# A hybrid decoder step on one core: modulation rows one unit sooner, last gate unit chunk by chunk, weight places in another order

## The reference

```
mod = silu(c) @ w_ada + b_ada                  # six pieces: shift, scale, gate, twice
h = rmsnorm(x) * (1 + sc1) + sh1
u, q, k, v, ga, gb = split(h @ w_in)
A = pool_mix(u) ; B = window_attention(q, k, v)
x = x + gt1 * ((sigmoid(ga) * (A @ w_a) + sigmoid(gb) * (B @ w_b)) @ w_out)
h2 = rmsnorm(x) * (1 + sc2) + sh2
x = x + gt2 * (relu(h2 @ w_up)**2 @ w_down)
y = rmsnorm(x)
```

## Time and profile before

| | |
|---|---|
| median of three runs | 1319.77 us |
| the profiled execution's own time | 1318.88 us |
| its span, first to last instruction | 1317.1 us |
| PE busy | 1278.0 us, 97% |
| DVE, ACT, POOL busy | 62%, 43%, 14% |
| mean granted PE clock | 0.993 of full speed |

### The profile page before, as it was taken

One profiled execution on the slowest core, in us unless ns is written; L12 is line 12 of the kernel. 1 busy time (PEld: TensorE's weight loads), 2 busy tenths in 40 slices (PEclk: granted clock), 3 DMA queues, 4 the chain that ended last, 5 costly groups with the idle time before them and its releaser, 6 DMA issues. The chain is left out here.

```text
span 1317.1 us, 24641 instructions
## 1 busy us (share of the span) xinstructions
PE 1278.0 (97%) x10185; PEld 1248.4 (95%) x10185; DVE 819.6 (62%) x1222; ACT 571.4 (43%) x984; POOL 189.1 (14%) x186
## 2 busy tenths in 40 slices
PE   6999999999999999998999999999999999999996
PEld 5899999999989999998889999999999999999996
DVE  7611446654333655347798877676768885688864
ACT  5322323454443633326666655555553434334332
POOL 1000100000000122222423332322320000000001
PEclk9999999999999999999999999999999999999999
DMA  9988422222222543543335554535398756676533
GB/s 308 317 275 277 152 65 66 72 86 71 66 66 74 175 132 102 153 141 111 94 121 156 163 161 154 164 123 158 122 335 250 250 179 234 213 222 207 181 129 100
DMA packets 238556, 211.59 MB, mean 161 GB/s; under 512 B 16145, under 2 KB 219797, under 8 KB 233565
## 3 DMA queue, kind: packets, MB, share of 16 engines
q1 hardware_dynamic: 237580, 209.66, 50.3%
q10 hardware_dynamic: 865, 0.36, 0.1%
HBM read 161.97 MB, written 49.04 MB: 160 GB/s over the span
## 5 line engine op out<-in xcount | busy, mean ns | idle before, releaser
L542 PE MATMUL psum<-xh,b_hi 128*128 128x264 f32 x908 | 257.9, 284 | 5.9 <-DVE b_lo L1658 3.6
L544 PE MATMUL psum<-xh,b_lo 128*128 128x264 f32 x908 | 257.9, 284 | 0.0
L543 PE MATMUL psum<-xl,b_hi 128*128 128x264 f32 x908 | 256.5, 282 | 0.0
L542 PE MATMUL psum<-dh,e_hi 128*128 128x264 f32 x896 | 255.3, 285 | 1.1 <-DVE e_lo L1658 1.0
L543 PE MATMUL psum<-dl,e_hi 128*128 128x264 f32 x896 | 254.0, 283 | 0.0
L544 PE MATMUL psum<-dh,e_lo 128*128 128x264 f32 x896 | 253.9, 283 | 0.0
L542 PE MATMUL psum<-h_hi,w_hi 128*128 128x384 f32 (+1 forms) x624 | 208.7, 334 | 5.2 <-DVE h_lo L1387 2.4
L543 PE MATMUL psum<-h_lo,w_hi 128*128 128x384 f32 (+1 forms) x624 | 202.1, 324 | 0.0
L544 PE MATMUL psum<-h_hi,w_lo 128*128 128x384 f32 (+1 forms) x624 | 201.9, 324 | 0.0
L542 PEld LDWEIGHTS psum<-xh,b_hi 128*128 128x128 f32 x908 | 170.5, 188 | 7.7 <-DVE b_lo L1658 4.9
L543 PEld LDWEIGHTS psum<-xl,b_hi 128*128 128x128 f32 x908 | 170.6, 188 | 0.0
(11 more groups left out here) (295 smaller groups left out, 2384.2 us busy)
## 6 DMA issues: line engine op xcount, KB each, us to landing
down_raw<-in_w_down_dram SPq DMA_DIRECT2D x72, 512.0 KB, 5.6
dr<-ff_scratch SPq DMA_DIRECT2D x28, 1056.0 KB, 8.3
up_raw<-in_w_up_dram SPq DMA_DIRECT2D x76, 256.0 KB, 3.8
ff_scratch<-st SPq DMA_DIRECT2D x64, 264.0 KB, 3.4
ada_p<-in_w_ada_dram SPq DMA_DIRECT2D x8, 2048.0 KB, 9.7
ff_scratch<-st SPq DMA_DIRECT2D x32, 396.0 KB, 3.5
w_raw<-in_w_in_dram SPq DMA_DIRECT2D x22, 512.0 KB, 5.2
gates_scratch<-g_out SPq DMA_DIRECT2D x16, 528.0 KB, 3.2
```

The lines of the kernel that those rows point to most:

```text
L542: mm(out, whi, rhi, start=first, stop=False)
L543: mm(out, whi, rlo, start=False, stop=False)
L544: return mm(out, wlo, rhi, start=False, stop=last)
```

## The change

**Start.** Pair 1's rows move from ahead of chunk 1 to between the two units of chunk 0, and their transpose moves to behind the first tile of the second unit. DVE's `by_token` steps are spread: two instead of three at first, then two, then one behind each lo. Of chunks 3 and 5 the normed value `nrm` is made by ACT (a new activation with the new semaphore `n_whole`) instead of DVE. ACT's row copies of pairs 1 to 3 stand ahead of chunks 2, 4 and 6 instead of 2, 3 and 5. The state row's transfer shares the semaphore of the vectors.

**Last gate unit.** `last_gate` goes chunk by chunk in the order 0, 4, 1, 5, 2, 6, 3, 7: six chunks through all three tiles, each with a signal `gate_left`, then the last two per tile. `turn_probs` stands behind the second chunk, `weigh` behind the fourth. ACT and DVE make the branch halves as the chunks of `h` become free, and ACT's three gate copies stand behind six of the eight hi copies.

**Weight places.** `down_place` exchanges the places 1 and 2 of the down weights.

```diff
+def down_place(k):
+    return (0, 2, 1, 3, 4)[k % 5]
+LAST_GATE = (0, 4, 1, 5, 2, 6, 3, 7)
+S_ORDER = (0, 1, 2, 4, 5, 6, 3, 7)
...
@@ PE, start @@
-                if k in (1, 2, 4):
+                if k in (2, 4):
                     pair_rows(k // 2 + 1)
                 for s in range(2):
+                    if (k, s) == (0, 1):
+                        pair_rows(1)
...
-                        if (s, t) == (0, 0) and k in (1, 2, 4):
+                        if (k, s, t) == (0, 1, 0):
+                            pair_turn(1)
+                        if (s, t) == (0, 0) and k in (2, 4):
                             pair_turn(k // 2 + 1)
@@ PE, last gate unit @@
+            def last_gate(i, u):
+                whi, wlo = weights(u)
+                for t in range(3):
+                    wait(pe, free[t], take(t, ("g", u, t)))
+                for n, k in enumerate(LAST_GATE[:6]):
+                    for t in range(3):
+                        last = mm3(psum[:, t, 0:TW[t]], ..., n == 0, False)
+                    last.then_inc(gate_left, 1)
+                    if n == 1:
+                        turn_probs(i, 1)
+                    if n == 3:
+                        weigh(i)
+                for t in range(3):
+                    for k in LAST_GATE[6:]:
+                        last = mm3(psum[:, t, 0:TW[t]], ..., False, k == LAST_GATE[7])
+                    last.then_inc(ready[t], 1)
...
@@ ACT, start @@
+                if k in (3, 5):
+                    act.wait_ge(h_done, k - 1)
+                    fn(nrm[:, k % 2, :], xn[:, k, 0:TP], ACT.Identity, scale=..., bias=...).then_inc(n_whole, 1)
@@ ACT, last gate unit @@
+            def branch_hi(k):
+                if k % 4 == 3:
+                    there(last_of[W_AB - 1])
+                else:
+                    act.wait_ge(gate_left, LAST_GATE.index(k % 4) + 1)
+                fn(hi, src, ACT.Copy).then_inc(s_hi_done, 1)
...
@@ DVE, start @@
-            for j in range(3):
+            for j in range(2):
                 by_token(j)
...
                 pair_add(p)
                 norm(2 * p)
-                norm(2 * p + 1)
+                if p == 3:
+                    norm(7)
                 norm_lo(2 * p)
                 norm_samples(p)
+                if p < 3:
+                    by_token(2 * p + 2)
                 norm_lo(2 * p + 1)
+                if p < 3:
+                    by_token(2 * p + 3)
@@ SP, down weights @@
-                        if up_place(m) // 2 == k:
+                        if up_place(m) // 2 == down_place(k):
                             when_released(*released(UP_RAW[m], False)[0:2])
```

More of the change, by code:

```diff
@@ L771, in pool_map @@
                     mm3(psum[:, t, 0:TW[t]], wp_hi[:, g, :], wp_lo[:, g, :], d_hi[:, cols(t)], d_lo[:, cols(t)], True, True).then_inc(ready[t], 1)
+            def last_gate(i, u):
[4 more added lines that the diff above has]
+                    for t in range(3):
+                        last = mm3(psum[:, t, 0:TW[t]], whi[:, k, :], wlo[:, k, :], h_hi[:, k, cols(t)], h_lo[:, k, cols(t)], n == 0, False)
+                    last.then_inc(gate_left, 1)
[5 more added lines that the diff above has]
+                    for k in LAST_GATE[6:]:
+                        last = mm3(psum[:, t, 0:TW[t]], whi[:, k, :], wlo[:, k, :], h_hi[:, k, cols(t)], h_lo[:, k, cols(t)], False, k == LAST_GATE[7])
+                    last.then_inc(ready[t], 1)
+                last_of[u] = ("g", u, 2)
             for i in range(BLK):
@@ L1011, in _ @@
                     split_hi(1)
+                if k in (3, 5):
+                    act.wait_ge(h_done, k - 1)
+                    fn(nrm[:, k % 2, :], xn[:, k, 0:TP], ACT.Identity, scale=gain1[:, k, 0:1], bias=mod[:, k, 0:1]).then_inc(n_whole, 1)
             split_hi(2)
@@ L1122, in gate_sig @@
                 fn(g_in[:, j % 2, :, :], g_in[:, j % 2, :, :], ACT.Sigmoid).then_inc(sig_done, 1)
-            there(last_of[W_AB - 1])
+            def branch_hi(k):
[3 more added lines that the diff above has]
+                    act.wait_ge(gate_left, LAST_GATE.index(k % 4) + 1)
+                hi, src = (a_hi[:, k, :], z[:, U0 + k, :]) if k < 4 else (o_hi[:, k - 4, :], z[:, Q0 + k - 4, :])
+                fn(hi, src, ACT.Copy).then_inc(s_hi_done, 1)
             for t in range(3):
                 freed(("pool", NG - 1, t))
-            for k in range(4):
-                fn(a_hi[:, k, :], z[:, U0 + k, :], ACT.Copy).then_inc(s_hi_done, 1)
-            freed(("o", BLK - 1))
-            for k in range(4):
-                fn(o_hi[:, k, :], z[:, Q0 + k, :], ACT.Copy).then_inc(s_hi_done, 1)
+            branch_hi(0)
+            pt_copy(BLK - 1, 1)
+            branch_hi(1)
+            done = there(("o", BLK - 1))
+            fn(z[:, Q0:Q0 + G, (BLK - 1) * P:TP], psum[:, 7, :].rearrange("p (c t) -> p c t", c=G), ACT.Copy).then_inc(done, 1)
+            branch_hi(2)
+            freed(("o", BLK - 1))
+            for k in (4, 5, 6):
+                branch_hi(k)
+            for t in range(3):
+                gate_copy(BLK - 1, 1, t)
+            for k in (3, 7):
+                branch_hi(k)
             split_hi(W_AB + 1)
@@ L1413, in _ @@
             norm_lo(1)
[L1414 removed]
+            for j in (2, 3):
                 by_token(j)
             for p in range(1, DK // 2):
[L1417 to L1419 removed]
                 pair_add(p)
                 norm(2 * p)
[L1422 removed]
+                if p == 3:
+                    norm(7)
                 norm_lo(2 * p)
                 norm_samples(p)
+                if p < 3:
+                    by_token(2 * p + 2)
                 norm_lo(2 * p + 1)
+                if p < 3:
+                    by_token(2 * p + 3)
             split_lo(2)
@@ L1553, in _ @@
                     nc.vector.tensor_copy(pool_tail[:, :, :].rearrange("p g (b r) -> p g b r", b=NB), pool_s[:, :, :, NT:PAD + NT]).then_inc(tail_done, 1)
-            for k in range(8):
-                dve.wait_ge(s_hi_done, k + 1)
+            for n, k in enumerate(S_ORDER):
+                dve.wait_ge(s_hi_done, n + 1)
+                if k % 4 == 3:
+                    there(last_of[W_AB - 1])
+                else:
+                    dve.wait_ge(gate_left, LAST_GATE.index(4 + k % 4) + 1)
                 src, hi, lo = (z[:, U0 + k, :], a_hi[:, k, :], a_lo[:, k, :]) if k < 4 else (z[:, Q0 + k - 4, :], o_hi[:, k - 4, :], o_lo[:, k - 4, :])
@@ L2194, in _ @@
                     if k < 3:
-                        at_step = max(released(UP_RAW[m], False)[2] for m in range(len(UP_RAW) - 6, len(UP_RAW)) if up_place(m) // 2 == k)
+                        at_step = max(released(UP_RAW[m], False)[2] for m in range(len(UP_RAW) - 6, len(UP_RAW)) if up_place(m) // 2 == down_place(k))
                     else:
```

31 lines of the change are left out of this document (19 added, 12 removed).

## The result

The changed kernel took **1309.91 us** (median of 4 runs, 1309.47 to 1311.97), the kernel before 1319.73 (4 runs, 1319.3 to 1321.25): ratio 0.9927, 95% interval 0.9909 to 0.9944. That is 9.8 us less; 7.2 were forecast. Run once more on another occasion the changed kernel took 1309.23 (five runs, 1309.03 to 1312.88). The profiled execution took 1309.54 us, its span 1307.7.

The account below looks back on a forecast made before the run. PE, busy 97% of the span, was taken as the bound, gaining only at waits and slow clock. Start 2.0 + last gate unit 4.2 + weight places 1.0 = 7.2 us: 1311.7 profiled, forecast median 1312.5, range 1310.5 to 1315.

Parts of the forecast that it names:

- range of 8 in 10: Whole kernel: the wider forecast range for the time, from 1309.9 to 1317.0 us.
- signs that would have shown it wrong: Pair 1 wait over 4 us, 1.2 GHz beyond 41.4, over 1 us wait at last gate unit or first product, feed-forward wait growing.
- The start: First units: 2.38 us wait at chunk 6 goes, 0.4 lost at pair 1's rows; 2.0 us gained, range 0.5 to 2.4.
- the other term: Start, pair 1's rows: PE waits 2.4 us instead of 0.94, chunk 1 starts late; 0.4 us lost.
- The case of a full clock: Start: if the clock were still full when pair 1's rows start, chunk 1 would start at 38.7.
- rival A: Start gives nothing: pair 1 lands late or its wait keeps the clock down; 1314.3 us, chance 0.16.
- D: Start: clock stays at 1.2 GHz through the chunks to 57.8, up to 19.8 us more; 1332 us, chance 0.05.
- The last gate unit: Behind the last gate unit: 2.81 us wait and slow clock go, 0.2 taken off; 4.2 us gained, range 1.5 to 4.5.
- Its two terms: Last gate unit: 2.81 us wait goes, and 3.2 us at 1.2 GHz did work of 1.6; together 4.4 us.
- Rival B: Behind last gate unit: gates return too late, PE waits 1.7 us for bank 3; 1314.0 us, chance 0.09.
- Rival C: Last gate unit: waits of 2 to 3 us return, clock falls again; gain 3.0 in all, 1316.8 us, chance 0.10.
- Weight places: Down product, second step: load issued earlier, PE's 1.02 us wait goes; 1.0 us gained, range 0 to 1.1.

Follow-up runs that it names:

- start_only: Kernel before with only the start's changes (pair 1's rows, by_token, nrm, row copies, joined semaphore): 1315.56 us, ratio 0.9970.
- halves_late: Changed kernel, ACT making all eight hi halves only after the last gate unit and gate copies, order 0, 1, 2, 4, 5, 6, 3, 7: 1316.04 us.
- busy_out: Changed kernel plus 28 identity transposes meant for the output product's wait, but placed where PE doesn't wait (524.34): 1314.06 us, ratio 0.9962.
- halves_plain: Changed kernel, all eight hi halves only after the last gate unit and gate copies, in order 0 to 7: 1313.53 us, ratio 0.9959.
- gate_only: Kernel before with only the last gate unit chunk by chunk and the branch halves in the places it leaves: 1314.05 us, ratio 0.9958.
- down_only: Kernel before with only places 1 and 2 of the down weights exchanged: 1318.16 us, ratio 0.9993.
- busy_out_2: Changed kernel plus 34 identity transposes inside PE's 3.97 us wait for wo_lo in the output product: 1311.93 us, ratio 0.9949.

## Why the prediction was right

The direction, the places and the mechanisms were right. The size was short by 2.6 us of 9.8 in the medians, and that the time still fell in the range of 8 in 10, by a hundredth of a us, is luck. None of the signs that would have shown it wrong came.

**The start: right in kind, too small (2.0 against 3.6).** The 2.38 us wait at chunk 6 went, by the chain the prediction named: the copy behind chunk 5's hi. With the copies put back it returns, as three smaller waits. The prediction put the lo's end at 56.5 and PE's need at 58.2; they were 54.85 and 56.66, the spare 1.8 as forecast. The failed size is the other term, 0.4 us lost at pair 1's rows: it was 0.75 gained at chunk 1, and 0.2 more with pair 1's turn, which is through by then. The wait ahead of them was 3.14 us, not 2.4, with the transfer landed at 34.2 instead of 33.8; but they ran in 1.95 us, not 3.24, because the clock was at 2.4 GHz where the prediction, from the earlier trace rows, had it at 1.2 until 38. The case of a full clock was also summed wrong, at 38.7 for chunk 1: half of the 3.24 and half of the 2.9 behind 33.8 give 36.9.

That the slow stretch would stay in its place rested on one execution. Of the seven profiled executions with the whole new start, five show no fall there, two a fall of 3.4 us right behind the wait for pair 1; of the three with the old start one shows 6.8 us and two 3.4. The traces tell how much of the 1.6 us not forecast is a matter of execution. The third unit begins at 62.0 to 63.8 in the seven, 62.8 in the mean, and at 64.8 to 66.0 in the three, 65.6 in the mean. So the start is worth about 2.8 us, half way between the forecast 2.0 and the 3.6 of the first pair of traces; the slow clock in that one execution of the kernel before makes up part of the rest. The median of start_only gives 3.8, its trace 2.6.

**Rivals A and D** speak of the clock at the start. A (no gain there, 1314.3) and D (slow clock through the chunks, 1332) did not come in the result, though the wait that was to cause them did, longer than forecast. The 3.4 us of slow clock of rival A did come in halves_late and busy_out; in halves_late it cost 1.3 us at the third unit (63.76 against 62.45).

**The last gate unit: right, 4.05 against 4.2.** The idle of 2.81 became 0.22, where the prediction had none, and the clock behind it is at 2.4 GHz. The 0.2 that it took off was for PE's wait for the bank of the first gate product; PE doesn't wait there. halves_plain gives 4.1 for the halves alone, the same number from the other side. Its two terms stand too: halves_late shows a wait of the same 2.81 without the fall, halves_plain with it. The first sigmoid came at 432.80. Before it was at 438.41; the shift of PE is 7.63, so against PE the gates are 2.0 us later. The prediction said 434.4, which with the start's further 1.6 is 432.8. Rival B needed PE to be ready for DVE before the gates are; the sigmoid ended at 434.77 and DVE took PE's bank at 435.59, so the bank was the later of the two by 0.8 us. Rival C needed holes of 2 to 3 us inside the unit; there are none.

**Weight places: right, 1.0 against 1.3.** The e_lo wait went, and 1.28 us with it: the wait of 1.02 and what PE takes to be back at its pace behind it. The load that was issued at 961.14 and took 12.3 us is now issued at 948.44, 12.7 us sooner, or 5 against PE's shift of 7.7. By issues (name, engine, KB, us to landing) it takes:

```profile
down_raw<-in_w_down_dram SPq DMA_DIRECT2D x1, 512.0 KB, 10.9
```

It lands at about 959.4, and its hi is made at 961.04. The 0.34 us at the first matmul of the down product are not part of it, as start_only and gate_only show. The Trainium skill, "DMA: Bandwidth & Descriptors", Queues, rings and completion order, has each engine take its descriptors in ring order, and the prediction read from it that what is passed gets later, without loss. The rows agree. The two transfers of 1056 KB that it passes are issued at 952.32 and 954.86 and take 10.4 and 10.5 us, to 962.7 and 965.4; before they were issued at 960.03 and 960.40 and landed at 969.5 and 972.1, which is 0.9 to 1.0 sooner once PE's shift of 7.7 is taken off. ACT first takes them up at 971.14, with no wait for them:

```profile
970.17 1.06 ACT L1244 ACTIVATE e_hi<-down_raw 128x1024 fp32r<-128x1024 f32 x1 [0.75 <-DMA down_raw<-in_w_down_dram]
971.14 1.07 ACT L1286 ACTIVATE dh<-dr 128x1056 fp32r<-128x1056 f32 x1
```

**The clock behind the output product.** The prediction let it cost 1 us either way. It costs nothing there: in the kernel before and in the changed one the second wait for wo_lo ends 9.14 us after the first (601.53 and 610.67; 593.90 and 603.04), with 3.4 us of slow clock in the one and 6.8 in the other. It is 9.14 or 9.15 in all 14 traces. Before:

```profile
601.53 0.59 PE L542 MATMUL psum<-mg,wo_hi 128*128 128x264 f32 x1 [3.97 <-DVE wo_lo L1315]
...
610.67 0.39 PE L542 MATMUL psum<-mg,wo_hi 128*128 128x264 f32 x1 [1.66 <-DVE wo_lo L1315]
```

**The sum.** 3.6 + 4.05 + 1.3 + 0.4 = 9.35 in the traces, and forecast 7.2: 1.6 too little at the start, 0.3 at the down weights, and 0.4 that belongs to no term, most of it a hold-up in the one execution of the kernel before.

## What to carry to other kernels

When an in-order engine has a short step that waits for another engine's result, look at what stands behind it whose inputs are ready: here the start's gain was gone when that step stood ahead of them again (3.8 to 4.5 us), and the more visible move beside it gave nothing. Operands that reuse the place of others can be made piece by piece if their last reader goes through its pieces in the order in which they are wanted next, but then the makers' order must match as well (the misplaced chunk 3 cost 2.4 us). Slow clock or idle time is worth something only if no fixed arrival comes behind it, so before filling a wait read the next one.

## What the runs showed of the hardware

- After a wait of one length the granted clock may fall or stay. Behind 2.81 us it fell in the kernel before, in start_only, in down_only and in halves_plain, and stayed in halves_late; behind the 3.14 us ahead of pair 1's rows it stayed, behind 2.81 us at that place in halves_late it fell:

```profile
34.60:37.90 3.30, 3.30 (x51) 0.50 1.05 329
```

- Back-to-back transposes of 128 columns kept the clock through a wait of 4 us in the one trace taken (busy_out_2), where it falls in all 13 others; 28 of them took 3.1 us where nothing hid them (busy_out, 524.22 to 527.32).
- A sigmoid may have its table loaded well before its data: the load ends at 429.27, the sigmoid starts at 432.80 with the data. No trace here shows a cost beside the 1.28 us; with the data there, the sigmoid starts 0.02 us behind the load's end (before, 438.39 and 438.41).
